# Output-projection weights and its first two tiles of rows fetched during the recurrence, their products placed between the pieces of its last state, TensorE two tiles ahead afterwards

## What is computed

```python
h = rms_norm(x, norm1_gain[l])
proj = h @ w_in[l]
...
sb_out = stick_breaking_attention(q, k, v)...
rw_out = rwkv7_time_mix(proj[..., SB_COLS:], ...)
mix = jnp.concatenate([sb_out, rw_out], axis=-1)
x = x + mix @ w_out[l]
h2 = rms_norm(x, norm2_gain[l])
x = x + hierarchical_moe(h2, w_router_group[l], w_router_expert[l], w_exp_gate[l], w_exp_up[l], w_exp_down[l])
```

## Time and profile before

| | before |
|---|---|
| median of 3 runs | 3054.91 us (3054.87 to 3056.44) |
| the profiled execution, its own time | 3058.22 us |
| its span, first to last instruction | 3056.5 us |
| mean granted TensorE clock | 0.975 |
| TensorE matmul busy | 2848.7 us (93%), 29606 records |
| VectorE busy | 1198.3 us (39%) |
| ScalarE busy | 999.0 us (33%) |
| GpSimd busy | 656.8 us (21%) |
| HBM read, written | 298.79 MB, 72.88 MB |

### The profile page before, as it was taken

One profiled execution on the slowest core, in us unless ns is written; L12 is line 12 of the kernel. 1 busy time (PEld: TensorE's weight loads), 2 busy tenths in 40 slices (PEclk: granted clock), 3 DMA queues, 4 the chain that ended last, 5 costly groups with the idle time before them and its releaser, 6 DMA issues. The chain is left out here.

```text
span 3056.5 us, 74180 instructions
## 1 busy us (share of the span) xinstructions
PE 2848.7 (93%) x29606; PEld 1673.3 (55%) x29607; DVE 1198.3 (39%) x2075; ACT 999.0 (33%) x1998; POOL 656.8 (21%) x857
## 2 busy tenths in 40 slices
PE   8999999999999997888888699968999999999998
PEld 3444444444666664777777545545555555555554
DVE  2333211113887875676666323342111111111111
ACT  1211100002666665554554323431222222222221
POOL 0000300000110113666566100002222222222222
PEclk9999999999999998999999799988999999999999
DMA  3212131112022010111110155423878678677763
GB/s 128 69 51 63 44 114 61 62 62 80 20 67 67 8 42 18 35 43 38 43 41 27 36 214 201 163 74 135 319 240 292 233 268 287 214 231 236 265 236 79
DMA packets 173682, 374.77 MB, mean 123 GB/s; under 512 B 28289, under 2 KB 109697, under 8 KB 154402
## 3 DMA queue, kind: packets, MB, share of 16 engines
q10 hardware_dynamic: 31088, 182.46, 15.3%
q1 hardware_dynamic: 129266, 146.25, 14.5%
q0 software_dynamic: 13120, 43.00, 6.7%
HBM read 298.79 MB, written 72.88 MB: 122 GB/s over the span
## 5 line engine op out<-in xcount | busy, mean ns | idle before, releaser
L2142 PE MATMUL gu_ps<-wg_,xT 128*64 128x384 f32 (+1 forms) x2592 | 574.5, 380 | 1.8 <-issue 1.8
L2143 PE MATMUL gu_ps<-wu_,xT 128*64 128x384 f32 (+1 forms) x2592 | 574.5, 380 | 0.0
L2142 PEld LDWEIGHTS gu_ps<-wg_,xT 128*64 128x64 f32 x2592 | 324.0, 137 | 280.6 <-issue 280.5
L711 DVE TENSOR_TENSOR_SCAN h_all<-h_all 128x512 f32<-128x512 f32 (+3 forms) x320 | 346.0, 1129 | 70.0 <-ACT h_all L663 43.4
L345 PE MATMUL front_ps<-low,high 128*128 128x512 f32 x768 | 336.6, 595 | 2.5 <-issue 2.5
L2143 PEld LDWEIGHTS gu_ps<-wu_,xT 128*64 128x64 f32 x2592 | 324.0, 137 | 0.0
L2163 PE MATMUL y_ps<-wd_,hT 128*64 128x512 f32 x648 | 295.4, 598 | 0.0
L2162 PE MATMUL y_ps<-wd_,hT 128*64 128x512 f32 x648 | 295.4, 598 | 0.0
L2237 DVE SCALAR_TENSOR_TENSOR h<-sil,gate,gu_ps 64x384 f32<-64x384 f32 (+1 forms) x162 | 78.9, 487 | 431.5 <-ACT sil L2194 431.5
L1754 PE MATMUL o_ps<-wo_sb,mixT_t 128*128 128x512 f32 x512 | 227.7, 599 | 19.0 <-DMA wo_sb<-in_w_out 19.0
L345 PEld LDWEIGHTS front_ps<-low,high 128*128 128x128 f32 x768 | 144.2, 191 | 172.8 <-issue 172.8
(11 more groups left out here) (311 smaller groups left out, 4567.0 us busy)
## 6 DMA issues: line engine op xcount, KB each, us to landing
wg_<-in_w_exp_gate ACTq DMA_DIRECT2D x29, 2048.0 KB
wu_<-in_w_exp_up ACTq DMA_DIRECT2D x29, 2048.0 KB
wd_<-in_w_exp_down ACTq DMA_DIRECT2D x29, 2048.0 KB, 18.8
pT<-low SPq DMA_DIRECT2D x13, 1024.0 KB, 3.9
rkv<-pT SPq DMA_DIRECT2D x96, 128.0 KB, 2.5
high<-in_x SPq DMA_DIRECT2D x16, 512.0 KB, 4.0
mixT_t<-mixT SPq DMA_DIRECT2D x16, 512.0 KB, 4.0
x_t<-in_x SPq DMA_DIRECT2D x16, 512.0 KB, 4.9
```

The costliest lines, as they stand in the source:

```text
L711: dve.tensor_tensor_scan(prod[:, n % KEPT, h, 0:w][:, ::-1], rows, rows, so_far, ALU.mult, ALU.bypass).then_inc(scanned, 1)
L2142: pe.matmul(gu_ps[half][LO, 0:wide], xT[:, k, :], wg[s][:, k, cols], start=(k == 0), stop=(k == KT - 1))
L2143: last = pe.matmul(gu_ps[half][HI, 0:wide], xT[:, k, :], wu[s][:, k, cols], start=(k == 0), stop=(k == KT - 1))
```

## The change

The projection's operands move into a part of SBUF, `high`, that the earlier stages use and the recurrence leaves free, and all stages up to routing share one PSUM tensor `ps` of eight banks, so that products can be made while the recurrence still runs. A new class `MixOut` holds the weights, the two slots for rows, the output banks 0 to 3 (the recurrence's X and Y) and the semaphores.

- SyncE's queue in the recurrence gets eight loads of 512 KB of `w_out` (one at the end of each of the steps 1 to 8), and at step 12 the rows of tiles 0 and 1 (512 KB each).
- TensorE's queue at n = 16 gets twelve parts of two products each, one behind every piece of the chain; the last four parts stand at n = 17, between `variance` and `gate` of state 15. Part 0 waits for X1_ready, the last inverse of state 15.
- In `mix_out_and_route` TensorE makes the products of tile t + 2 around the work of tile t. SyncE starts with x of tiles 0 and 1, the router weights, the gain, and 2 MB of expert weights; behind these come the rows of tile 2. Rows and x have semaphores of their own; VectorE waits for x. The rows of t + 2 are fetched once the products of t are made.
- Smaller edits: `root` shares the tile of `sq`; two semaphores (scores1_done, scores2_done) become one that counts both; the third slot of expert weights lies in `high` instead of a tile of its own.

```diff
@@ time_mixing, SyncE
+                    if 1 <= n <= KT:
+                        mix.load_weights(sp, n - 1)
+                    if n == NG + 4:
+                        sp.wait_ge(stored[0], (NG // 2 + 1) * 16)
+                        for t in range(2):
+                            mix.load_rows(sp, t, t)
@@ time_mixing, TensorE
+                def mix_rows(part):
+
+                    s, half, k = part // 8, part // 4 % 2, part % 4 * 2
+                    if part == 0:
+                        pe.wait_ge(mix.weights, 16 * KT)
+                        pe.wait_ge(X1_ready, STEPS * NL)
+                    if part % 8 == 0:
+                        pe.wait_ge(mix.loaded[s], 16)
+                    mix.products(pe, s, half, (k, k + 1))
...
                     if there(b):
                         from_state(b, 0)
+                    if n == STEPS:
+                        mix_rows(0)
...
                     if there(b):
                         solve(b, 0)
+                    if n == STEPS:
+                        mix_rows(1)
...
                     if there(t):
                         variance(t, m)
+                    if n == STEPS + 1:
+                        for part in range(12, 16):
+                            mix_rows(part)
...
@@ MixOut
+    def products(self, pe, s, half, ks):
+        for k in ks:
+            done = pe.matmul(self.ps[:, s, half, :], self.rows[:, s, k, :], self.w[:, k, half * 512:(half + 1) * 512],
+                             start=(k == 0), stop=(k == KT - 1))
+        if half == 1 and k == KT - 1:
+            done.then_inc(self.mixed, 1)
@@ mix_out_and_route, SyncE
-                w_out_v = w_out[0].rearrange("(k p) c -> p k c", p=P)
                 load(0, 0)
-                for half in range(2):
-                    sp.dma_start(w_sb[:, :, half * 512:(half + 1) * 512], w_out_v[:, :, half * 512:(half + 1) * 512]).then_inc(w_out_loaded[half], 16)
                 load(1, 1)
...
                     for s in range(2):
                         t = i * 2 + s
+                        sp.wait_ge(mixed, t + 1)
+                        mix.load_rows(sp, t + 2, s)
                         store(t, s)
@@ mix_out_and_route, TensorE
                 def one_tile(t, s, n, first, last):
-                    if not last:
-                        mix(t + 1, 1 - s, n + s, 0)
+                    more = not (isinstance(t, int) and t >= NT - 2)
+                    if more:
+                        mix_half(t + 2, s, n + 1, 0)
...
-                    if not last:
-                        mix(t + 1, 1 - s, n + s, 1)
+                    if more:
+                        mix_half(t + 2, s, n + 1, 1)
...
-                for half in range(2):
-                    pe.wait_ge(w_out_loaded[half], 16)
-                    mix(0, 0, 0, half)
```

136 lines of the change are left out of this document (86 added, 50 removed).

## The result

The changed kernel takes 3063.64 us (median of 11 runs) against 3054.91 us of before (11 runs beside them): the ratio is 1.0031, with a 95% interval of 1.0021 to 1.0040. It is slower, by 6 to 12 us, where 6.2 us less were forecast. Against the 0.2% that the prediction took as the border, the lower end of the interval lies just outside.

What follows compares the result with a forecast made beforehand. TensorE was taken to bound the stage except at its ends. +12.3 + 1.5 - 9.6 - 10.4 = -6.2 us took the profiled 3058.2 to 3052.0, so the median to 3048.7 us; range 3043 to 3057.5.

Steps and rivals of the forecast that it cites:

- The last state, +12.3 us: Last inverse to last `output_and_state`: eleven parts at 1.94 us fill TensorE's queue, ending at 1751.0 against 1738.7; +12.3 us.
- The last step, +1.5 us: Last `output_and_state` to outp: the norm now waits for the gate behind the last parts, 11.8 us against 10.3; +1.5 us.
- The start of mixing out, -9.6 us: Border to tile work: first product 15.1 us after the first transfer, work beginning at 17.1 instead of 26.7; -9.6 us.
- In between, 0: Middle of mixing out: fourteen tiles keep their 16.84 us period, with rows fetched in time; 0.
- the end, -10.4 us: End of mixing out: no products left after tile 13's logits, 25.5 us to the totals against 35.9; -10.4 us.
- Loads during the recurrence, root on sq, the merged semaphore, other addresses: 0: Recurrence: loads and small edits cost 0; if the cover fails, a state's inputs come 1.4 us late once per step.
- The prediction's own sign of being wrong: End of the recurrence, forecast near 1751: the forecast is wrong if it comes before 1748 or after 1756.
- The rival for "slower": Last state: TensorE's clock stays at 0.50; until 1739 gives +3.6 us, 3058.5; to the end, over 3080; chance 0.09.
- the products hide as meant: Last state and border: tile 2's rows overtake expert weights, perhaps crossings free; -11.6 us or more, 3043.3; chance 0.12.
- Crossings cost more: Last state: twelve parts alone between pieces cost 0.5 us more each; -0.2 us, 3054.7; chance 0.17.
- Nothing happens: Recurrence: no effect since w_out and the rows are loaded late; chance 0.02.

Runs made afterwards that it cites:

- spread: Against the change with w_out loaded ahead of the recurrence: 12 products in the last state instead of 24, 8 at mixing out's start; 3042.64 us, ratio 0.9963.
- the run with the rows first: The change with each part of the first experts' weights asked for behind the second tile of its pair; 3063.0 us, ratio 1.0038 to the kernel before.
- doubled: The change with two w_out loads in each of steps 1 to 8, each slice fetched twice; 3071.33 us, ratio 1.0069 to the kernel before.
- the burst: The change with all eight w_out loads issued together in step 5 of the recurrence; 3052.17 us, ratio 1.0012 to the kernel before.
- loads only: The change with w_out and first rows still fetched in the recurrence, but all products made at mixing out's start; 3069.72 us, ratio 1.0048 to before.
- edits only: The change with w_out, the rows of tiles 0 and 1 and all products moved to mixing out's start; 3065.28 us, ratio 1.0044 to before.

## Why the prediction was wrong

It gave 3048.7 us and a range to 3057.5; 3063.64 came. Point by point:

- *The last state, +12.3 us:* measured 31.82 - 20.86 = +11.0. The model of a full queue was right, part for part (1.91 us against 1.94), and the clock rose about as assumed (0.89 on average from 1730 to 1740, 1.00 behind). A crossing cost 0.17 to 0.20 us in before, the change and spread. The rule of the Trainium skill that the prediction names (TensorEngine Tiling (Array Packing), Tiling Modes: changing the tiling mode drains TensorE) agrees in that the change of mode had a price.
- *The last step, +1.5 us:* 1774.13 - 1762.55 = 11.6 us, +1.2.
- *The start of mixing out, -9.6 us:* the first product came after 15.9 us, 15.1 were said. The wait for w_out was replaced by a longer one for the rows behind the expert weights, and the run with the rows first confirmed the cause by removing 4.9 us of it. From the first transfer to the totals written the stage is 19.2 us shorter (298.1 before, 278.9 after); less the end's 10.2 that is -9.0 for the start.
- *In between, 0, and the end, -10.4 us:* tile period 16.84 us, 25.7 us at the end where 25.5 were said; 35.9 before.
- These five terms sum to the forecast -6.2 us, and the trace gives -6.7 (334.84 against 328.16 us from the last inverse to the first operation behind the totals).
- *"Loads during the recurrence, root on sq, the merged semaphore, other addresses: 0":* **this is the step that failed**, by +12.9 us in the profiled executions, and the loads in the steps are its cause (14 to 21 us in the profiles of three kernels that have them, gone in the one that loads first, which is 9 us faster by the ratios). I had looked for the cover of the loads in the queue of the state's inputs, which are fetched a step ahead, and said what it would cost if that cover failed: 1.4 us a step. The inputs were indeed in time: no engine waits for one. That 8 x 1.4 us come near the 12.9 measured is luck. What was not in the list was TensorE's own instructions, which come over the same DMA engines; the profile of before had shown both signs, the queue "q8 instruction" on its page and 35 us of TensorE's waits under "issue" in a stage that is written out step by step. The prediction's own sign of being wrong, a recurrence that ends after 1756, came true for this reason: it ended at 1762.55, from a last inverse at 1730.73.
- The rival for "slower" was the clock at 0.50 in the filled state. It didn't come true there: the clock was 1.00 from 1740 on. Its mechanism, that TensorE goes on at the lower clock behind a stand, did act, but in the steps ahead and behind the lengthened waits. Rival "the products hide as meant", with rows that overtake: no, and the rule of the Trainium skill that was weighed against it (DMA: Bandwidth & Descriptors, Queues, rings and completion order: a ring's descriptors are consumed in order) agrees with the 4.9 us that the product gained once the expert weights stood behind the rows. "Crossings cost more": no, 0.18 us. "Nothing happens": no.
- The range failed with it: it was built from the spreads of the terms that had a size, and the term set to 0 brought none.

## What to carry to other kernels

In this kernel, a stage that is unrolled and keeps TensorE on small matmuls was fed with instructions through the same DMA engines as the data. Before a transfer is called hidden in such a stage, add up TensorE's waits by "issue" there, and try the transfer where TensorE waits for something else anyway, or all at once, or in small pieces; the 512 KB in each step was the dear form. A chain with short gaps takes as much foreign work as its gaps hold (here about one product at a place), and what goes beyond lengthens it; the rest belongs at the borders of the stages, where TensorE stands. At a border, ask which transfer ends the wait and what is queued ahead of it: moving 2 MB that nobody needs yet from in front of 0.5 MB made the stage 5 us shorter in the profile.

## What was unexpected of the hardware

- TensorE's instructions arrive in packets of 16 KB, and TensorE goes on about 2.5 us behind the start of a late one (1302.7 and 1305.16 in the change; 1369.97 and 1372.53 in doubled; 1392.76 and 1395.16 in the burst).
- With a single load of 0.5 MB in the DMA engines a packet of instructions started 2.2 us later than without it, as the load's last bytes went. Here two queues of different kinds, q1 and q8, met in the same DMA engines. The trace shows the packet's start, not when it was asked for. The Trainium skill (DMA: Bandwidth & Descriptors, Queues, rings and completion order) says that a DMA engine takes turns between its queues packet by packet. The burst agrees, since a packet of q8 started among its bytes; the single and the double load, behind which it started only at the end, don't show such turns.
- Behind a wait of TensorE of 3.7 us inside a busy stretch the mean granted clock was 0.58 for 3 us, and behind one of 4.75 us it was 0.50 for 2 us:

```profile
1370.00:1372.00 2.00, 0.00 (x0) 0.00 (x0) 0.00 (x0) 0.00 (x0) 0.00 (x0) 0.98 0.05 11
1372.00:1374.00 2.00, 1.47 (x28) 1.47 (x30) 0.00 (x0) 0.00 (x0) 0.00 (x0) 0.50 0.03 10
```

  These are stretches of doubled, TensorE's busy time first, its granted clock third from the end. In the change, this second price is smaller than the first, the longer stand: TensorE is busy 433.0 us up to the last inverse, against 431.3 and 429.3 in the two profiles of before, and stands 92.7 us against 81.6 and 82.0 (the stretches from 1205 us). In loads only, against edits only, the two are nearer: 9.8 us busy longer and 13.1 us more of standing.
- The profile's releaser of a wait for two things can be the wrong one by several us: the page gave the border's 20 us to an addition that ended at 1793.4, and the run that moved the rows alone removed 5 us of them.
